# The parameter chain and the tables of the state-space mixer, moved to other places of layer 0

## What is computed

```python
def s5_mixer(u, a_re, a_im, b_re, b_im, c_re, c_im, d_skip, log_step, w_glu):
    lam = lax.complex(jnp.minimum(a_re.astype(F32), -1e-4), a_im.astype(F32))
    step = jnp.exp(log_step.astype(F32))
    a_bar = jnp.exp(lam * step)
    b_bar = ((a_bar - 1.0) / lam)[..., None] * lax.complex(b_re.astype(F32), b_im.astype(F32))
    bu = jnp.einsum('blgc,gpc->blgp', uf.astype(jnp.complex64), b_bar)
    ...                      # states: scan over the 256 tokens with a_bar
    y = jnp.einsum('blgp,gcp->blgc', states, c_mat).real + d_skip.astype(F32) * uf

def sq_relu_mlp(xn, w1, w2):
    return jnp.square(jax.nn.relu(xn @ w1)) @ w2
...
for layer in range(DEPTH):
    h = h + mixer(rmsnorm(h, norm_mix[layer]), ...)
    h = h + cross_attention(rmsnorm(h, norm_xattn[layer]), memn, ...)
    h = h + sq_relu_mlp(rmsnorm(h, norm_mlp[layer]), mlp_w1[layer], mlp_w2[layer])
```

## Time and profile before

| | us |
|---|---|
| median of three executions | 2604.4 |
| lowest and highest | 2603.81, 2612.93 |
| span of the profiled execution | 2608.9 |
| PE busy | 2511.2 (96%) |
| DVE busy | 1421.0 (54%) |
| ACT busy | 1170.2 (45%) |
| POOL busy | 355.8 (14%) |

### The profile page before, as it was taken

One profiled execution on the slowest core, in us unless ns is written; L12 is line 12 of the kernel. 1 busy time (PEld: TensorE's weight loads), 2 busy tenths in 40 slices (PEclk: granted clock), 3 DMA queues, 4 the chain that ended last, 5 costly groups with the idle time before them and its releaser, 6 DMA issues.

```text
span 2608.9 us, 30798 instructions
## 1 busy us (share of the span) xinstructions
PE 2511.2 (96%) x11785; PEld 2069.2 (79%) x11785; DVE 1421.0 (54%) x1622; ACT 1170.2 (45%) x1533; POOL 355.8 (14%) x503
## 2 busy tenths in 40 slices
PE   7979999999889999999999997999999999999997
PEld 5858887778667888888888885678888888888886
DVE  4525553355896555555555534256655555555555
ACT  5634444345534444444445433345644444444444
POOL 2773310020472000000000117000000000000000
PEclk9989999999999999999999998999999999999999
DMA  8545553454557655665565664665456655665563
GB/s 282 194 144 174 198 178 129 146 180 152 177 189 254 194 184 189 190 192 183 188 192 184 203 210 138 194 224 198 142 197 191 193 188 184 191 193 187 184 193 113
DMA packets 261041, 483.64 MB, mean 185 GB/s; under 512 B 18301, under 2 KB 41909, under 8 KB 260565
## 3 DMA queue, kind: packets, MB, share of 16 engines
q1 hardware_dynamic: 242548, 453.35, 54.0%
q0 software_dynamic: 4256, 17.03, 2.1%
q10 hardware_dynamic: 14144, 12.00, 1.4%
HBM read 464.54 MB, written 21.99 MB: 186 GB/s over the span
## 4 chain that ended last, share of the span: by engine, by line
PE 86%; POOL 5%; DVE 5%; issue 2%; ACT 1%; DMA 1%; SPq 0%; ACTq 0%; DVEq 0%; POOLq 0%
PE acc L526 26%; PE acc L528 25%; PE acc L527 25%; POOL arena L2083 5%; PE at L579 4%; PE tp L555 2%; DVE wlo L1586 1%; DMA arena<-in_mem 1%; PE tp L579 1%; PE acc L821 1%; PE acc L819 1%; PE acc L820 1%; DVE h L1620 0%; ACT whi L1060 0%; DVE arena L1666 0%
## 5 line engine op out<-in xcount | busy, mean ns | idle before, releaser
L1586 DVE TENSOR_TENSOR wlo<-raw,whi 128x1024 fp32r<-128x1024 f32 x824 | 1039.4, 1265 | 1055.2 <-ACT whi L1060 1053.2
L1060 ACT ACTIVATE whi<-raw 128x1024 fp32r<-128x1024 f32 x824 | 871.3, 1061 | 1066.6 <-PE acc L528 1034.4
L526 PE MATMUL acc<-whi,xt_hi 128*128 128x512 f32 x1760 | 698.0, 397 | 3.5 <-DVE wlo L1586 1.9
L528 PE MATMUL acc<-whi,xt_lo 128*128 128x512 f32 x1760 | 689.0, 391 | 0.0
L527 PE MATMUL acc<-wlo,xt_hi 128*128 128x512 f32 x1760 | 688.9, 391 | 0.0
L526 PE MATMUL acc<-whi,yt_hi 128*128 128x512 f32 x1472 | 581.3, 395 | 5.2 <-DVE yt_lo L1727 4.2
L528 PE MATMUL acc<-whi,yt_lo 128*128 128x512 f32 x1472 | 575.8, 391 | 0.0
L527 PE MATMUL acc<-wlo,yt_hi 128*128 128x512 f32 x1472 | 575.3, 391 | 0.0
L526 PEld LDWEIGHTS acc<-whi,xt_hi 128*128 128x128 f32 x1760 | 332.8, 189 | 76.6 <-issue 4.8
L528 PEld LDWEIGHTS acc<-whi,xt_lo 128*128 128x128 f32 x1760 | 332.1, 189 | 70.3
L527 PEld LDWEIGHTS acc<-wlo,xt_hi 128*128 128x128 f32 x1760 | 332.9, 189 | 66.5
(11 more groups left out here) (199 smaller groups left out, 1292.3 us busy)
## 6 DMA issues: line engine op xcount, KB each, us to landing
raw<-in_mlp_w SPq DMA_DIRECT2D x256, 1024.0 KB, 5.3
raw<-in_ab_w_in SPq DMA_DIRECT2D x56, 1024.0 KB, 5.0
raw<-in_cd_w_in SPq DMA_DIRECT2D x32, 1024.0 KB, 5.7
raw<-in_xa_wkv SPq DMA_DIRECT2D x16, 1024.0 KB, 9.2
raw<-in_ab_w_out SPq DMA_DIRECT2D x16, 1024.0 KB, 5.0
raw<-in_cd_w_out SPq DMA_DIRECT2D x16, 1024.0 KB, 6.9
raw<-in_xa_wq SPq DMA_DIRECT2D x8, 1024.0 KB, 5.1
ca_d<-arena ACTq DMA_DIRECT2D x16, 288.0 KB, 3.3
```

The costliest lines, as they stand in the source:

```text
L526: pe.matmul(a, xh, whi[:, w, kk], start=opens and kk == 0, stop=False)
L528: last = pe.matmul(a, xl, whi[:, w, kk], start=False, stop=closes and kk == 1)
L1060: act.activation(split_weights(whi, kind, i), half_weights(raw, kind, i), ACT.Copy)\
L1586: dve.tensor_tensor(split_weights(wlo, kind, i), half_weights(raw, kind, i), split_weights(whi, kind, i).bitcast(F32), ALU.subtract).then_ ...
```

## The change

1. The 15 small transfers leave the start. POOL issues them behind layer 0's output projection's first block, where `prep` was loaded back before. `prep_d` and both its transfers, and the waits for them on ACT and DVE, are gone.
2. `s5_rows` (PE), the copies out of PSUM (ACT, 3 slots later), the reciprocal (DVE) and the sine (ACT) move from the four memory units into chunk 0 of layer 0's MLP (`ROWS_T` = 8, `SIN_T` = 29), and POOL's chain with them. POOL reaches `load_decay` and `rotary` with nothing before them but `tri` and `wff`.
3. The tables move out of chunk 0. Chunks 5 and 6 are written out instead of being trips of the loop (`TAB_CHUNKS`), and the groups stand three halves apart, `CHUNK_T = [3 * k]`, over 46 of their 64 halves.
4. The views `par`, `craw` and `ptmp` move to parts of the arena that are free in the MLP.

```diff
-        prep = view(4480, 3136)
-        par = view(9664, 16 * 32, "p (k q) -> p k q", k=16)
+        par = view(2048, 16 * 32, "p (k q) -> p k q", k=16)
...
-        CHUNK_T = [k * 27 // 15 for k in range(16)]
+        TAB_CHUNKS = (5, 6)
+        CHUNK_T = [3 * k for k in range(16)]
         DVE_T = [t + 2 for t in CHUNK_T]
+        ROWS_T, SIN_T = 8, 29
...
+            def s5_params(t):
+                if t == ROWS_T:
+                    assert p.n["at"] == at_before_rows
+                    s5_rows()
...
-                    if u == 1 and i == 3:
-                        s5_rows()
...
-                step(True, False)
-                with pe.Fori(0, CHUNKS - 2) as r:
+                step(True, False, params)
+                with pe.Fori(0, trips) as r:
                     p.enter(r, dict(STEP_RATES, his=0))
                     step(False, False)
-                    p.leave(CHUNKS - 2)
+                    p.leave(trips)
+                for k in range(len(apart)):
+                    step(False, False, tables, 32 * k)
                 step(False, True)
...
-            def s5_param(t):
-                if t == 14:
+            def s5_params(t):
+                if t == ROWS_T + 3:
                     at_copy(lambda bank: [(par[:, 0:3, :].rearrange("p k q -> p (k q)"), bank[:, 0:96])])
...
-                if t == 29:
+                if t == SIN_T:
                     act.wait_ge(s5_par, 1)
                     act.activation(par[:, par_of["sin"], :], par[:, par_of["th"], :], ACT.Sin)
...
+            def s5_params(t):
+                if t == 0:
+                    p.bump("at", 3)
+                if t == SIN_T - 1:
+                    dve.wait_ge(s5_lam, 1)
+                    dve.reciprocal(par[:, par_of["t2"], :], par[:, par_of["t1"], :]).then_inc(s5_inv, 1)
...
                 if k == 0:
-                    dve.wait_ge(prep_in, 16)
+                    dve.wait_ge(prep_done, 1)
                     dve.wait_ge(tab_zero, 1)
...
-            for n in (1, 2):
-                pool.wait_ge(at_free[n % 2], n // 2 + 1)
-            pool.dma_start(prep_d, prep).then_inc(prep_out, 16)
...
-            pool.dma_start(prep, prep_d).then_inc(prep_in, 16)
```

More of the change, by code:

```diff
@@ L905, in up_after, with step @@
                         transpose_block(nat, y_tok, up_after.kt)
-                def step(first, last):
+                def step(first, last, beside=None, t0=0):
                     def u_after(u):
@@ L914, in after @@
                                 up_after(i)
-                            if first:
-                                tables(8 * u + i)
+                            if beside:
+                                beside(t0 + 8 * u + i)
                         return after
@@ L1312, in _ @@
             for e in range(len(E_UNITS)):
[L1313 to L1317, removed]
+                unit("full", lambda i, e=e: even_slots(e, i))
             def out_slots(n, i):
@@ L1394, in attention_and_out, with mlp, step @@
                 unit("mixed", slot)
-            def mlp(layer, row, next_row, final, tables=lambda t: None):
-                def step(first, last):
+            def mlp(layer, row, next_row, final, params=None, tables=None):
+                apart = TAB_CHUNKS if tables else ()
+                trips = CHUNKS - 2 - len(apart)
+                def step(first, last, beside=None, t0=0):
                     def slot_of(u):
                         def slot(i):
-                            if first:
-                                tables(8 * u + i)
+                            if beside:
+                                beside(t0 + 8 * u + i)
                             if u in (1, 2):
@@ L1422, in step @@
                         unit(kind, slot_of(u))
-                step(True, False)
-                with act.Fori(0, CHUNKS - 2) as r:
+                step(True, False, params)
+                with act.Fori(0, trips) as r:
                     p.enter(r, dict(STEP_RATES, hid=0, **{f"slab{b}": 4 for b in range(RING)}))
                     step(False, False)
-                    p.leave(CHUNKS - 2)
+                    p.leave(trips)
+                for k in range(len(apart)):
+                    step(False, False, tables, 32 * k)
                 step(False, True)
@@ L1876, in attention_and_out, with mlp, step @@
                 unit("mixed", slot)
-            def mlp(layer, m, next_row, final, tables=lambda t: None):
-                def step(first, last):
+            def mlp(layer, m, next_row, final, params=None, tables=None):
+                apart = TAB_CHUNKS if tables else ()
+                trips = CHUNKS - 2 - len(apart)
+                def step(first, last, beside=None, t0=0):
                     def slot_of(u):
@@ L1913, in step @@
                         unit(kind, slot_of(u))
-                step(True, False)
-                with dve.Fori(0, CHUNKS - 2) as r:
+                step(True, False, params)
+                with dve.Fori(0, trips) as r:
                     p.enter(r, dict(STEP_RATES))
                     step(False, False)
-                    p.leave(CHUNKS - 2)
+                    p.leave(trips)
+                for k in range(len(apart)):
+                    step(False, False, tables, 32 * k)
                 step(False, True)
```

152 lines of the change are left out of this document (75 added, 77 removed).

## The result

The changed kernel takes 2584.5 us (median of four, 2582.6 to 2585.8), the kernel before beside it 2608.6 (2603.8 to 2612.9; four executions here, where the forecast started from the median of three, 2604.4). The ratio is 0.990, from 0.988 to 0.993. In a later series, with six against eleven executions, it was 0.9915, from 0.990 to 0.993. The forecast was 2603.0, from 2586 to 2614: no measurable change. The time was missed by 18.5 us and the range by 1.5, both on the fast side.

A forecast was written before the change was run, and what follows sets the result against it. PE's work plus its gaps was taken to bound the kernel. The terms -20.8 (stop), -9.0 (start), +0.8 (chain), -50.6 (chunk 0) and +78.2 us (chunks 5 and 6) sum to -1.4: median 2603.0, range 2586 to 2614.

The forecast's parts named there:

- a delay that was read in the old one: Chunks 5 and 6: POOL, released by `ca_d` about 6.2 us behind PE's group, slows DVE's group; PE's waits 37.3 us.

## What to carry to other kernels

When work is moved to another rhythm, don't carry over a delay that was read in the old one: ask what else has a period there (here a slab every two halves), and work the delay out for each phase. Where a moved piece waits for an engine, its slot on that engine is worth more than its place in the program: the place cost 8 us here (58.4 less 50.6), one half of slot won 28. A short rule for a delay can fit the mean because its errors cancel, so try it on single waits. Two parts of a change can have opposite signs, so price and try them apart. And give the range a term for the scatter of the clock outside the change.

## What the runs showed of the hardware

- DVE's tensor-tensor instructions of 128x256 took 0.42 us with POOL idle and twice that, 0.75 to 0.97, beside POOL's; its pair of small copies 0.36 and 0.69 to 0.94, and its split of a half (128x1024) 1.23 and up to 1.84 (changed kernel).
- `ca_d` (288 KB) and its two neighbours let POOL start 4.6 us behind PE's group with 0.07 MB of the weights' queue beside them, and 8.7 with 1.1 MB. A transfer on ACT's queue pays for a slab on SP's that it doesn't depend on.
- The same program had 208.1 us in one execution and 212.8 in another for the same attention part, by low-clock stretches alone.
